# Second layer of a two-block model: gate units among the later heads, products of two units dealt out, and the GLU's first chunks in another order

## The reference, cut to what matters

```python
def odd_mixer(h, w_in, conv_w, conv_b, w_rg, b_rg, w_ig, b_ig, lam, w_out):
    p = jnp.einsum("btd,dn->btn", h, w_in)
    xr, gate = jnp.split(p, [W_LRU], axis=-1)
    xc = causal_depthwise_conv(xr, conv_w, conv_b)          # 4 taps
    xh = xc.reshape(bsz, t, LRU_HEADS, LRU_HD)
    r = jax.nn.sigmoid(jnp.einsum("bthi,hij->bthj", xh, w_rg) + b_rg)
    i = jax.nn.sigmoid(jnp.einsum("bthi,hij->bthj", xh, w_ig) + b_ig)
    log_a = -LRU_C * r * jax.nn.softplus(-lam)
    a = jnp.exp(log_a)
    bterm = jnp.sqrt(-jnp.expm1(2.0 * log_a)) * (i * xc)
    _, hs = lax.associative_scan(_lin_combine, (a, bterm), axis=1)
    return jnp.einsum("btn,nd->btd", hs * jax.nn.silu(gate), w_out)

# in s5_mixer, behind the state space part:
y = jax.nn.gelu(y)
ab = y @ w_glu
return ab[..., :dm] * jax.nn.sigmoid(ab[..., dm:])
```

## Time and profile before

| | |
|---|---|
| median of 3 runs | 1719.36 us |
| the profiled execution | 1718.13 us, its span 1716.2 us |
| TensorE busy | 1691.8 us, 99% of the span |
| VectorE, ScalarE, GpSimd busy | 51%, 44%, 56% |
| granted TensorE clock | 0.999 of full |
| odd layer's X, R and G units | from 330 to 492 us of the span |
| GLU's first products | from 639 us |

### The profile page before, as it was taken

How to read it: one execution, slowest core, us unless ns; L and a number is a source line. 1 busy time by engine, 2 the same in 40 slices (tenths; PEclk the granted TensorE clock), 3 DMA queues, 4 the chain that set the end, 5 groups by cost and what they waited for, 6 DMA issues and landing times.

```text
span 1716.2 us, 20954 instructions
## 1 busy us (share of the span) xinstructions
PE 1691.8 (99%) x8056; PEld 1396.0 (81%) x8056; DVE 869.2 (51%) x1250; ACT 762.9 (44%) x1203; POOL 969.3 (56%) x606
## 2 busy tenths in 40 slices
PE   9999999999999999999999999999999999999998
PEld 7888888777778898888888888888678888888887
DVE  3999997757787785522212121386644221212124
ACT  5333325466867773343222222454765332323234
POOL 5858755657678565654444444664547444444464
PEclk9999999999999999999999999999999999999999
DMA  4322323222245234222222222223112222222221
GB/s 170 105 99 87 111 99 115 95 74 95 89 162 211 68 128 136 99 91 95 97 98 99 98 98 98 86 98 99 47 47 93 98 99 98 98 92 95 97 99 62
DMA packets 56258, 172.65 MB, mean 101 GB/s; under 512 B 6496, under 2 KB 14816, under 8 KB 55264
## 3 DMA queue, kind: packets, MB, share of 16 engines
q1 hardware_dynamic: 56160, 171.33, 29.5%
HBM read 165.01 MB, written 6.29 MB: 100 GB/s over the span
## 4 chain that ended last, share of the span: by engine, by line
PE 70%; DVE 5%; ACT 3%; issue 2%; POOL 1%; DMA 1%; SPq 0%; DVEq 0%; ACTq 0%
PE B L315 57%; PE B L1687 1%; PE B L2439 1%; PE B L2441 1%; PE B L2437 1%; PE B L2235 1%; PE B L2335 1%; PE B L2314 1%; DVE SW L1150 1%; PE B L298 1%; DVE B L1016 1%; PE B L1614 1%; PE B L1579 1%; PE B L300 1%; PE B L299 1%
## 5 line engine op out<-in xcount | busy, mean ns | idle before, releaser
L291 POOL TENSOR_TENSOR WL<-RAW,WH 128x1024 fp32r<-128x1024 f32 x281 | 681.8, 2428 | 613.6 <-ACT WH L287 613.3
L287 ACT ACTIVATE WH<-RAW 128x1024 fp32r<-128x1024 f32 x281 | 296.5, 1057 | 627.3 <-PE B L315 593.8
L315 PE MATMUL B<-P0h,WH 128*128 128x512 f32 x1096 | 428.1, 391 | 3.7 <-ACT WH L287 1.9
L315 PE MATMUL B<-P0l,WH 128*128 128x512 f32 x1096 | 421.9, 390 | 1.3 <-DVE P0l L432 1.3
L315 PE MATMUL B<-P0h,WL 128*128 128x512 f32 x1096 | 276.4, 389 | 0.0
L315 PEld LDWEIGHTS B<-P0h,WH 128*128 128x128 f32 x1096 | 205.7, 188 | 48.4 <-DVE Yl L428 2.6
L315 PEld LDWEIGHTS B<-P0l,WH 128*128 128x128 f32 x1096 | 205.8, 188 | 44.4 <-DVE P0l L432 2.3
L315 PEld LDWEIGHTS B<-P0h,WL 128*128 128x128 f32 x1096 | 205.7, 188 | 42.7
L439 DVE TENSOR_TENSOR H<-H,B 128x512 f32<-128x512 f32 x88 | 60.2, 686 | 288.3 <-PE B L315 288.2
L1967 DVE SCALAR_TENSOR_TENSOR TMP<-B,RS 128x512 f32<-128x512 f32 x64 | 44.1, 691 | 258.5 <-PE B L315 244.1
L315 PE MATMUL B<-P1h,WH 128*128 128x512 f32 x448 | 174.7, 390 | 0.0
(11 more groups left out here) (354 smaller groups left out, 2668.8 us busy)
## 6 DMA issues: line engine op xcount, KB each, us to landing
RAW<-in_w SPq DMA_DIRECT2D x281, 512.0 KB, 3.2
PX<-in_zeros SPq DMA_DIRECT2D x4, 1024.0 KB, 10.0
H<-in_xT SPq DMA_DIRECT2D x8, 256.0 KB, 4.8
U<-u SPq DMA_DIRECT2D x32, 64.0 KB, 2.0
g<-GB SPq DMA_DIRECT2D x8, 256.0 KB, 2.1
GB<-g SPq DMA_DIRECT2D x32, 64.0 KB, 2.0
out<-Q SPq DMA_DIRECT2D x4, 512.0 KB, 3.6
CA<-in_zeros SPq DMA_DIRECT2D x1, 1920.0 KB, 10.0
```

The lines of the kernel that those rows point to most:

```text
L287: act.activation(WH[:, i % NS, :], RAW[:, i % NR, :], ACT.Copy).then_inc(*inc("w_hi", i))
L291: pool.tensor_tensor(WL[:, i % NS, :], RAW[:, i % NR, :], WH[:, i % NS, :].bitcast(F32), ALU.subtract).then_inc(*inc("w_lo", i))
L315: return pe.matmul(b[:, :], w[:, ws[c]], x[:, c, :], start=start, stop=stop)
```

## The change

In ODD, G0 to G3 move forward among X7 to X11. In an R unit, each gate's three products are followed by two products of the unit that comes next (pe_beside, a generator); the rest of that unit follows after the last gate. The sums of the odd layer's norm move from between X0 and X1 to behind the second chunk of X1. ScalarE makes the high half of the weights two places behind an R unit ahead of the sigmoids, not behind them. pe_glu_start waits for the banks and the low halves of all three units first, and then goes through the chunks in an outer loop and through the units in an inner one.

```diff
--- before.py
+++ after.py
@@ -46,7 +46,7 @@
 
 EVEN = ("G0 A0 G1 A1 B0 B1 B2 B3 G2 A2 G3 A3 S0 S1 S2 S3 P0 B4 B5 G4 A4 G5 A5 B6 S4 B7 S5 S6 S7 "
         "G6 A6 G7 A7 P1 F0 F1 F2 F3 F4 F5 F6 F7 K0 K1 K2 K3 K4 K5 K6 K7 O0 O1 O2 O3 O4 O5 O6 O7").split()
-ODD = ("X0 X1 X2 X3 X4 R0 X5 X6 X7 X8 X9 X10 X11 R1 G0 G1 G2 G3 G4 G5 R2 G6 G7 G8 G9 G10 G11 "
+ODD = ("X0 X1 X2 X3 X4 R0 X5 X6 G0 X7 G1 X8 X9 R1 G2 X10 G3 X11 G4 G5 R2 G6 G7 G8 G9 G10 G11 "
        "O0 O1 O2 O3 O4 O5 O6 O7 Q0 Q1 Q2 Q3").split()
 EVEN = [(x[0], int(x[1:])) for x in EVEN]
 ODD = [(x[0], int(x[1:])) for x in ODD]
@@ -796,6 +796,29 @@
     rbanks = Banks([])
     rbanks.bank = banks.bank
 
+    def pe_beside(pe, what, freed_by):
+
+        i = IDX[what]
+        wh, wl = weights(i)
+        b, before = banks.take(what, freed_by)
+        pe.wait_ge(*at(*before))
+        pe.wait_ge(*at("w_hi", i))
+        for c in range(8):
+            ws = slice(128 * c, 128 * c + 128)
+            pe.matmul(b[:, :], wh[:, ws], P0h[:, c, :], start=c == 0, stop=False)
+            yield
+            pe.matmul(b[:, :], wh[:, ws], P0l[:, c, :], start=False, stop=False)
+            yield
+        pe.wait_ge(*at("w_lo", i))
+        for c in range(8):
+            last = pe.matmul(b[:, :], wl[:, 128 * c:128 * c + 128], P0h[:, c, :], start=False, stop=c == 7)
+            if c == 7:
+                last.then_inc(*inc("unit", what))
+            yield
+
+    def odd_bank_free(kind, c):
+        return "x_lo", ("xc" if kind == "X" else "y", c)
+
     def pe_odd(pe):
         for _ in range(2):
             rbanks.queue.append(banks.queue.popleft())
@@ -803,14 +826,18 @@
             what = odd_what(n)
             i = IDX[what]
             wh, wl = weights(i)
-            if kind in "XG":
-                linear(pe, what, P0h, P0l, range(8), ("x_lo", ("xc" if kind == "X" else "y", c)), "odd" if n == 0 else None)
+            if kind in "XG" and kind_at(n - 1) == "R":
+                pass
+            elif kind in "XG":
+                linear(pe, what, P0h, P0l, range(8), odd_bank_free(kind, c), "odd" if n == 0 else None,
+                       {1: lambda: stat_sums(pe, "odd", pool=rbanks)} if n == 1 else {})
             elif kind == "O":
                 if c == 0:
                     banks.queue.extend(rbanks.queue)
                 linear(pe, what, Yh, Yl, range(8), "h", "y" if c == 0 else None)
             elif kind == "R":
                 pe.wait_ge(*at("w_lo", i))
+                beside = pe_beside(pe, odd_what(n + 1), odd_bank_free(*ODD[n + 1]))
                 for h in range(4 * c, 4 * c + 4):
                     pe.wait_ge(*at("x_lo", ("xc", h)))
                     for j, r in enumerate("ri"):
@@ -819,6 +846,10 @@
                         ws = slice((h % 4) * 256 + 128 * j, (h % 4) * 256 + 128 * j + 128)
                         last = mm3(pe, b[:, :], wh[:, ws], wl[:, ws], Yh[:, h, :], Yl[:, h, :], True, True)
                         last.then_inc(*inc("unit", what if (h % 4, j) == (3, 1) else (r, h)))
+                        for _ in range(2):
+                            next(beside)
+                for _ in beside:
+                    pass
             else:
                 if c == 0:
                     for b in CB:
@@ -837,9 +868,7 @@
                     last.then_inc(*inc("unit", what if j else ("q4", 2 * c)))
                     if (c, j) == (3, 0):
                         pe_square_sums(pe, (4, 5))
-            if (kind, c) == ("X", 0):
-                stat_sums(pe, "odd", pool=rbanks)
-            elif (kind, c) == ("X", 1):
+            if (kind, c) == ("X", 1):
                 stat_spread(pe, "odd", pool=rbanks)
 
     def unit_key_ri(r, h):
@@ -906,6 +935,7 @@
                     for h in pair(r, d == 3):
                         lru_exp(act, h)
             if kind == "R":
+                highs(act, IDX[what] + 3)
                 act_gates(act, pair(c, 0))
                 act_parts(act, n - 1)
                 if kind_at(n - 1) == "X":
@@ -913,7 +943,6 @@
                 act_gates(act, pair(c, 1))
                 if kind_at(n - 1) == "G":
                     act_first(act, n - 1)
-                highs(act, IDX[what] + 3)
                 act_parts(act, n)
                 highs(act, IDX[what] + 4)
             elif kind_at(n + 1) != "R":
@@ -1804,19 +1833,18 @@
     def pe_glu_start(pe, chunks):
 
         for what in GLU[:3]:
-            i = IDX[what]
-            wh, wl = weights(i)
             if chunks[0] == 0:
                 _, before = banks.take(what, "evac_a" if what[2] > 7 else "evac_d")
                 pe.wait_ge(*at(*before))
-                pe.wait_ge(*at("w_lo", i))
-            b = banks.bank[what]
-            for c in chunks:
-                pe.wait_ge(*at("g_lo7" if c == 7 else "g_lo", ("g", c)))
-                ws = slice(128 * c, 128 * c + 128)
-                last = mm3(pe, b[:, :], wh[:, ws], wl[:, ws], P0h[:, c, :], P0l[:, c, :], c == 0, c == 7)
-            if chunks[-1] == 7:
-                last.then_inc(*inc("unit", what))
+                pe.wait_ge(*at("w_lo", IDX[what]))
+        for c in chunks:
+            pe.wait_ge(*at("g_lo7" if c == 7 else "g_lo", ("g", c)))
+            ws = slice(128 * c, 128 * c + 128)
+            for what in GLU[:3]:
+                wh, wl = weights(IDX[what])
+                last = mm3(pe, banks.bank[what][:, :], wh[:, ws], wl[:, ws], P0h[:, c, :], P0l[:, c, :], c == 0, c == 7)
+                if c == 7:
+                    last.then_inc(*inc("unit", what))
 
     def pe_glu(pe):
         pe_glu_start(pe, range(7, 8))
```

## The result

The changed kernel takes 1726.09 us in the median of 6 runs (1725.09 to 1727.66), the kernel before 1719.2 us in the runs beside it: a ratio of 1.004 with a 95% interval of 1.003 to 1.005. Forecast were 1723.9 us and a range up to 1727.0.

A forecast was written before the change was run, and what follows sets the result against it. In the layer the prediction took the chain through ScalarE and VectorE as the bound, not TensorE's stalls. Layer +1.8 and GLU start +2.7 gave +4.5 us on 1719.36, so 1723.9 us; range 1718.5 to 1727.0.

The forecast's parts named there:

- Part 1: Norm's sums inside X1: X1 ends 0.95 us earlier, bounds 0 and 0.99.
- Leg A: Second layer, R0's start to R1's first sigmoid: 48.2 us instead of 48.58, -0.4.
- B: Second layer, R1's first sigmoid to lru input 4: 17.6 us instead of 18.44, -0.9.
- leg C: Second layer, lru input 4 to R2's first sigmoid: 25.1 us instead of 22.28, +2.8.
- Leg D: Second layer, R2's first sigmoid to the low half of y6 and G10's start: +1.2 us.
- Sum of the layer: At G10's start, sums and four legs together: +1.8 us, bounds -10.5 and +3.1.
- Part 3: GLU start, chunks outermost: output delayed 4.05 us by waiting, chunk 6 stall of 1.16 gone; net +2.7 us.
- rival 3: TensorE's clock falls behind one of the long waits, slowing GLU products: 1727 us; chance 0.10.
- 1, that the stalls just go: Second layer's TensorE stalls (10.5 us) vanish; with the GLU wait -7.8, 1711.6 us; chance 0.08.
- 2, that only the GLU costs: R2's sigmoids come in time, layer ends at -0.5; sum +2.2, 1721.5 us; chance 0.22.
- 4, that the GLU start gains: GLU start gains 1.2 us, its third low half coming before TensorE does: 1720.0 us; chance 0.04.

The follow-up runs named there:

- e5: Kernel before with only the norm's sums moved behind the second chunk of X1: 1717.14 us against 1719.39 (0.9989).
- e4: e1 with the units in their old order, keeping sums in X1, dealt-out products and early high half: 1719.46 us against 1718.13 of the kernel before (1.0004).
- e7: e1 with X11 right behind X10, so three G units lie between X11 and R2: 1721.62 us in one run.
- e9: e1 with the dummy sigmoid and its table load ahead of the last split before R1 and R2: 1719.0 us against 1719.39 of the kernel before (0.9993).
- e11: e4 with the high half back behind the sigmoids: 1720.71 us against 1719.26 of the kernel before (1.001).
- e10: e6 plus the early high half of weights in R0 and R2, not R1; no dealing out, old order: 1714.92 us against 1719.26 of the kernel before (0.9976).
- e1: Changed kernel with the GLU start as before, so the layer part alone: 1720.61 us against 1718.13 of the kernel before (1.0013).
- e3: Changed kernel with 20 small dummy products on TensorE during the GLU wait (records show 40): 1725.07 us, 1.0 less than the changed kernel.
- e2: Kernel before with only the new pe_glu_start: 1723.53 us against 1718.13 (1.003).
- e6: e5 with GLU chunks outermost only behind output 7, units outermost with their own waits before it: 1717.04 us against 1719.39 of the kernel before (0.9984).

## Why the prediction was right, and where it was short

- **Part 1, the sums (forecast -0.95).** Right: -0.87 from the mark to R0, and e5 shows the same alone, in the total too.
- **Legs A, B and C (-0.4, -0.9, +2.8).** Right, each within 0.2: -0.3, -0.7, +2.8. The cause of leg C is shown by e4 (order back: 22.41), e7 (VectorE's total, not its last piece) and e9 (the table load is on the chain: 23.60). TensorE's stalls came where the legs put them.
- **Leg D (+1.2).** Measured +1.6, with two errors against each other. The gates took 8.89 us, not 7.4, since the clock fell behind R2's wait: e4 without that fall has 7.48. This is +1.4. And the s5 products to G10 took 17.24, not 18.4: I had called that stretch VectorE without a gap, and it is, but its work got shorter. The first s5 product took 1.91 us before, while GpSimd made two low halves, and 0.68 after, when the first of them had been made during R2. The high half that now comes early is the cause: e11 has the dealing out but not the early high half, and the product takes 1.90 us; e4 has both, and it takes 0.68. e10 shows it without dealing: 17.23, and leg D 27.9.
- **Sum of the layer (+1.8).** Measured +2.6 from the mark to O0, and in e1 2.7. Without the fall behind R2 it is +1.2, as in e1's total, so the sum was 0.6 too high. VectorE's s5 stretch got 1.1 us shorter, and the other legs came out some tenths longer than forecast.
- **Part 3, the GLU start (+2.7).** The wait was 4.25 us, the chunk 6 stall went and chunk 7 came in time. From output 6 to the first linear unit 27.90 us passed against 23.49, +4.4: 2.8 for the wait (e3 has 26.31) and 1.6 for the clock.
- **The clock.** This is the step that was too small: the sum has it at nothing, and I put all of it into rival 3 with a chance of 0.10. In the profile it fell three times, behind R2's wait, among the Q units at 552 us, and behind the GLU wait. The second costs 1.6 us and the third 1.6 (e3 shows the third). Profile: the mark is 0.5 earlier, 2.6 for the layer, 1.6 for the second fall, 4.4 for the GLU, together 8.1, which is 1724.3 - 1716.2. By the granted clocks of the runs, the changed kernel has two to four falls and the kernel before none to two. The 1.2 us that I added because the median of before stood above its profile was such a fall as well: its profile had none, and 1719.4 is its time with one.
- **Rivals.** 1, that the stalls just go: refuted; R2's third group waited 3.57 us. 2, that only the GLU costs: refuted by e1. 4, that the GLU start gains: refuted by e2, yet e6 shows that its second half alone does gain 1.3 us. 3, the clock: this is what happened, and on top of the forecast's mechanism. The measured 1726.09 lies outside the forecast's own range (1722.3 to 1725.5) and close to rival 3's 1727. Its price was a guess, though: one fall at 3.1 us, where in the median there were two more falls than before, at some 1.6 each. That the two agree is luck. What the forecast did price, +4.5, came out at +4.3 with the same number of falls. The rule of the Trainium skill (TensorE: Matmul & The Clock Gate, Part 1: The HAM clock gate) holds here in its direction behind the two long waits: idle, then 1.2 GHz, shown by 0.67 and 0.72 granted over the stretches at 454 and 646 us. The fall at 552 us had no such wait ahead of it.
- **Small slips in the sums.** Leg A's steps add up to 48.0, not 48.2, and 4.41 - 0.33 is 4.08, not 4.05. Neither changes the forecast.

What stays open is why the clock fell at 552 us. No wait over 0.3 us stands there; before it TensorE had 8 tiny products of two columns (16 in the records) for 1.9 us, and in the profile of the kernel before the same place kept its clock. Other experiments had it too (e2, e4, e9, e10) or not (e1, e3, e5, e6, e7, e11). Nor does the length of a wait alone decide: in e4 the clock fell behind 1.87 us, and in e11 it stayed full behind 2.64 us.

## What to carry to other kernels

A stall on the busiest engine is not always time that can be won: find out which chain releases it, and measure that chain from milestone to milestone; work that is put into the stall helps only if it does not delay the chain. When several waits are gathered ahead of a loop, the last of them decides when the first product runs, so put each wait in front of the first instruction that needs it. A wait of a few us on TensorE cost some 1.6 us more when the clock fell behind it. Filler products kept it up in e3, but the wait itself stayed; e6 has neither.

## What the runs showed of the hardware

- A fall of the clock cost some 1.6 us of dense products. It occurred behind waits of TensorE of 4.25, 3.57, 3.08 (e7), 2.39 (e11), 2.03 (e9) and 1.87 us (e4), in one place with no wait of note, and in e1's profile 8 us behind the start. The times of the kernel before stand in steps of 1.5 to 1.7 us by it.
- The same VectorE product of 128x512 took 1.91 us beside GpSimd's low halves, and 0.68 us without them. The product behind it ran beside a low half in every kernel, and took 2.9 us.
- A function table load of ScalarE took 1.28 us each time; it cost nothing where ScalarE waited for something else (e9).
